# Recurrence stages: GpSimd makes two of the first query products, the state's blocks get banks of their own, and the modulation tiles move between the levels

## The reference

```python
def gla_chunk(q, k, v, logf, s0):
    ...
    b = jnp.cumsum(logf, axis=2)
    decay = jnp.where(mask, jnp.exp(jnp.where(mask, diff, 0.0)), 0.0)
    att = jnp.einsum('bnthk,bntshk,bnshk->bnhts', q, decay, k)
    o_intra = jnp.einsum('bnhts,bnshv->bnthv', att, v)
    ...
    def step(s, xs):
        o = jnp.einsum('bchk,bhkv->bchv', qc, s)
        s = dc[..., None] * s + jnp.einsum('bchk,bchv->bhkv', kc, vc)

def hgrn2_mix(q, iv, zf, zb, g, lbf, lbb, s0f, s0b):
    logf_f, k_f = forget_terms(zf, lbf)
    o_f, s_f = gla_chunk(q, k_f, iv, logf_f, s0f)
    logf_b, k_b = forget_terms(zb, lbb)
    o_b, s_b = gla_chunk(flip(q), flip(k_b), flip(iv), flip(logf_b), s0b)
    o = o_f + flip(o_b)
    ...

# per layer l:  (context rows first, then the latent rows, which start from the context's final states)
mod_x = (cond_x @ w_mod[l] + b_mod[l])[:, None, :]
yc, s_f, s_b = token_mixer(hc, ..., zero_state, zero_state, seq_conv)
yx, _, _ = token_mixer(hx, ..., s_f, s_b, latent_conv)
```

## Time and profile before

| | us |
|---|---|
| median of 3 runs | 4057.24 |
| the profiled execution's own time | 4046.82 |
| its span | 4045.0 |
| first recurrence | 226.5 to 275.2 |
| second recurrence | 275.2 to 338.3 |
| third recurrence | 2104.2 to 2161.4 |

### The profile page before, as it was taken

The page is one execution under the profiler, slowest core; times in us unless marked ns, Lnnn a source line. Parts: engine busy times, 40 slices in busy tenths (PEclk is TensorE's granted clock), DMA queues, the critical chain, the costliest instruction groups (busy, mean ns, idle before and its releaser), DMA issues. The chain is left out here.

```text
span 4045.0 us, 42202 instructions
## 1 busy us (share of the span) xinstructions
PE 3271.7 (81%) x13636; PEld 2079.7 (51%) x13636; DVE 2453.7 (61%) x5321; ACT 1372.9 (34%) x2942; POOL 1675.2 (41%) x1761
## 2 busy tenths in 40 slices
PE   6977986777777776677887777676779999999999
PEld 4845732223223332222576522232248978888788
DVE  4365746656556566665365755565557667676575
ACT  3364311112111111111365211111135566555664
POOL 0020566666666666666131566666630030000300
PEclk8989998888888888899998898898889999999999
DMA  5253699999999999999344899999964525455254
GB/s 194 104 220 124 228 365 354 371 364 363 368 359 361 372 361 365 353 365 378 135 157 167 325 376 353 377 358 364 372 247 176 207 84 188 177 181 202 84 188 146
DMA packets 247946, 1095.56 MB, mean 271 GB/s; under 512 B 28337, under 2 KB 31793, under 8 KB 228529
## 3 DMA queue, kind: packets, MB, share of 16 engines
q0 software_dynamic: 221184, 805.40, 51.8%
q1 hardware_dynamic: 26544, 287.47, 19.5%
HBM read 1091.72 MB, written 1.05 MB: 270 GB/s over the span
## 5 line engine op out<-in xcount | busy, mean ns | idle before, releaser
L2087 PE MATMUL ps<-v_rows,diagonal 128*128 128x512 f32 x3072 | 1542.4, 655 | 593.1 <-issue 271.0
L2087 PEld LDWEIGHTS ps<-v_rows,diagonal 128*128 128x128 f32 x3072 | 617.5, 209 | 1496.6 <-issue 1230.2
L1960 DVE CUSTOM_DVE_ANT_0 u_rows<-u_rows,ps 128x1024 f32<-128x1024 f32 x768 | 921.8, 1220 | 676.9 <-DMA u_rows<-in_u,experts 394.7
L1932 POOL DMA_INDIRECT v_rows<-in_v,experts x768 | 728.7, 949 | 482.0 <-issue 215.1
L1922 POOL DMA_INDIRECT u_rows<-in_u,experts x768 | 734.5, 956 | 341.9 <-issue 234.5
L2006 ACT ACTIVATE hidden<-hidden 128x2 f32<-128x2 f32 x384 | 77.5, 203 | 1716.0 <-DVEq L1962 865.7
L2842 PE MATMUL ps<-h_high_low,weights_high 128*128 128x512 f32 x1408 | 499.5, 400 | 6.5 <-DVE h_high_low L2697 6.3
L3265 DVE TENSOR_TENSOR weights_low<-ring,weights_high 128x1024 fp32r<-128x1024 f32 (+1 forms) x328 | 402.9, 1240 | 2.7 <-ACT weights_high L3258 2.5
L2843 PE MATMUL ps<-h_high_low,weights_low 128*128 128x256 f32 x1408 | 395.2, 281 | 0.0
L3258 ACT ACTIVATE weights_high<-ring 128x1024 fp32r<-128x1024 f32 (+1 forms) x328 | 338.7, 1033 | 99.7 <-PE ps L2843 54.1
L2842 PEld LDWEIGHTS ps<-h_high_low,weights_high 128*128 128x128 f32 x1408 | 265.4, 188 | 74.0 <-DVE h_high_low L2697 6.2
(11 more groups left out here) (357 smaller groups left out, 4029.1 us busy)
## 6 DMA issues: line engine op xcount, KB each, us to landing
ring<-in_ffn_gu SPq DMA_DIRECT2D x44, 2048.0 KB, 8.3
ring<-in_w_in SPq DMA_DIRECT2D x26, 2048.0 KB, 8.2
ring<-in_w_mod SPq DMA_DIRECT2D x24, 2048.0 KB, 9.5
ring<-in_ffn_down SPq DMA_DIRECT2D x32, 1408.0 KB, 6.0
ring<-in_peer_wq SPq DMA_DIRECT2D x8, 2048.0 KB, 8.6
u_rows<-in_u,experts POOLq DMA_INDIRECT x768
v_rows<-in_v,experts POOLq DMA_INDIRECT x768
ring<-in_w_out SPq DMA_DIRECT2D x4, 2048.0 KB, 10.2
```

The source lines that it names most:

```text
L1932: pool.indirect_dma_start(self.VROWS[n % self.v_slots][:, :], None, m.dram["v"], bass.IndirectOffsetOnAxis(ap=self.IDX[:, n:n + 1], axis=0 ...
L1960: dve.tensor_tensor_reduce(rows[:, :], rows[:, :], self.rows(), 1.0, 0.0, ALU.mult, ALU.add, self.HID[:, t % 2, s + r:s + r + 1])
L2087: mm = pe.matmul(self.A.ps[:, self.Y_BANK + half, :], self.DIAG[:, (g % DIAGONALS) * GROUP + r, :], rows[:, half * 512:(half + 1) * 512], ...
```

## The change

The line numbers of the changed kernel are up to 20 higher than those of the kernel before.

1. `first_vector` keeps two of its four query products on DVE (buffer 0). The two for buffer 1 become `first_copy`, which POOL makes ahead of its totals. ACT waits for them (`first_copied`) ahead of merge 1.
2. `FinalState` writes its turned rows to banks 1, 2, 3 and 7 and the state to banks 1 and 3. Its parts are placed apart: on PE the transposes open the stage, the state's products come behind level 1; on ACT `first_scalar` comes first, then the row copies, and the state is copied behind merge 2. PE waits for the copied state ahead of the final pass and no longer ahead of level 1.
3. `MOD_LEVELS` goes from (-1, -1, 1, 3, 4, 6, 7) to (-1, 0, 2, 4, 5, 7, 8).
4. ACT copies the modulation row behind the attention's last copy, and PE turns it behind the final pass (into bank 5, before bank 2).

```diff
-MOD_LEVELS = (-1, -1, 1, 3, 4, 6, 7)
+MOD_LEVELS = (-1, 0, 2, 4, 5, 7, 8)
...
+    TURN_BANKS = (1, 2, 3, 7)
+    STATE_BANKS = (1, 3)
...
-    def tensor(self, pe):
+    def tensor_rows(self, pe):
...
         mm.then_inc(m.e_turned.sem, 1)
+
+    def tensor_state(self, pe):
+        m, A = self.m, self.A
         pe.wait_ge(m.e_kept.sem, self.kept + 1)
...
     def gpsimd(self, pool, m):
 
+        self.first_copy(pool)
+        pool.drain().then_inc(m.first_copied.sem, 1)
         for level in range(1, LEVELS):
...
     def first_vector(self, dve):
         if self.queries:
-            for buf, right, d in ((0, 0, 1), (0, 1, 0), (1, 0, 0), (1, 1, 1)):
+            for buf, right, d in ((0, 0, 1), (0, 1, 0)):
                 dve.tensor_tensor(self.halves(self.QX[:, 1, buf, :, :], 1)[right], self.halves(self.q, 1)[right],
+                                  self.halves(self.total(1, d), 1)[right], ALU.mult)
+
+    def first_copy(self, eng):
+        if self.queries:
+            for right, d in ((0, 0), (1, 1)):
+                eng.tensor_tensor(self.halves(self.QX[:, 1, 1, :, :], 1)[right], self.halves(self.q, 1)[right],
                                   self.halves(self.total(1, d), 1)[right], ALU.mult)
...
         def _(act):
             if final is not None:
-                final.scalar_rows(act)
+                final.rows_turned(act)
             tree.first_scalar(act)
             act.drain().then_inc(m.act_a.sem, 1)
             if final is not None:
-                final.scalar_state(act)
+                final.scalar_rows(act)
             act.activation(G, G, ACT.Silu)
...
                 tree.pool_merged(act, m, level)
+                if level == 1:
+                    act.wait_ge(m.first_copied.sem, m.first_copied.at(1))
...
-                if level == LEVELS:
-                    beside.scalar(act)
+                if final is not None and level == 2:
+                    final.scalar_state(act)
...
             act.drain().then_inc(m.act_c.sem, 1)
+            beside.scalar(act)
...
             if final is not None:
-                final.tensor(pe)
+                final.tensor_rows(pe)
...
-                if final is not None and level == 1:
-                    final.ready(pe)
...
                 mm.then_inc(m.pe_a.sem, 1)
+                if final is not None and level == 1:
+                    final.tensor_state(pe)
                 beside.products_at(pe, level)
-            beside.turn(pe)
             pe.wait_ge(m.act_c.sem, m.act_c.at(1))
             if STATE is not None:
+                final.ready(pe)
...
             mm.then_inc(m.pe_b.sem, 1)
+            beside.turn(pe)
```

More of the change, by code:

```diff
@@ L1185, in tensor @@
                 n = 2 * dh + half
-                mm = pe.transpose(A.ps[:, 4 + n // 4, (n % 4) * P:(n % 4 + 1) * P], self.E[:, dh, half * P:(half + 1) * P],
+                mm = pe.transpose(A.ps[:, self.TURN_BANKS[n // 4], (n % 4) * P:(n % 4 + 1) * P], self.E[:, dh, half * P:(half + 1) * P],
                                   A.const[:, C_IDENT:C_IDENT + P])
         mm.then_inc(m.e_turned.sem, 1)
+    def tensor_state(self, pe):
+        m, A = self.m, self.A
         pe.wait_ge(m.e_kept.sem, self.kept + 1)
@@ L1192, in tensor, with rows_turned @@
             for half in range(2):
-                mm = pe.matmul(A.ps[:, 6 + dh // 4, (dh % 4) * P:(dh % 4 + 1) * P], self.KR[:, 2 * dh + half, :],
+                mm = pe.matmul(A.ps[:, self.STATE_BANKS[dh // 4], (dh % 4) * P:(dh % 4 + 1) * P], self.KR[:, 2 * dh + half, :],
                                self.IV[:, 2 * self.s + half, h * P:(h + 1) * P], start=(half == 0), stop=(half == 1))
         mm.then_inc(m.state_made.sem, 1)
+    def rows_turned(self, act):
+        act.wait_ge(self.m.e_turned.sem, self.turned + 1)
     def scalar_rows(self, act):
         m, A = self.m, self.A
-        act.wait_ge(m.e_turned.sem, self.turned + 1)
         for b in range(4):
-            act.activation(self.KR[:, 4 * b:4 * b + 4, :], A.ps[:, 4 + b, :].rearrange("p (n c) -> p n c", n=4), ACT.Copy)
+            act.activation(self.KR[:, 4 * b:4 * b + 4, :], A.ps[:, self.TURN_BANKS[b], :].rearrange("p (n c) -> p n c", n=4), ACT.Copy)
         act.drain().then_inc(m.e_kept.sem, 1)
@@ L1207, in scalar_state @@
         for b in range(2):
-            act.activation(self.STATE[:, 4 * b:4 * b + 4, :], A.ps[:, 6 + b, :].rearrange("p (n c) -> p n c", n=4), ACT.Copy)
+            act.activation(self.STATE[:, 4 * b:4 * b + 4, :], A.ps[:, self.STATE_BANKS[b], :].rearrange("p (n c) -> p n c", n=4), ACT.Copy)
         act.drain().then_inc(m.state_kept.sem, 1)
@@ L1529, in _ @@
             mm.then_inc(m.pe_b.sem, 1)
+            beside.turn(pe)
     m.totals.passed(LEVELS - 1)
+    m.first_copied.passed(1)
     m.merged.passed(LEVELS - Tree.POOL_FROM)
@@ L1617, in mixer @@
                     with ExitStack() as inner:
-                        beside = Modulation(m, A, BESIDE_MOD[layer][s], inner, bank=0, spot=2)
+                        beside = Modulation(m, A, BESIDE_MOD[layer][s], inner, bank=0, spot=5)
                         recurrence_stage(m, A, s, tree, IV, ATN, ATD, ATO, final, part(MIXR, 0, s), part(Q, 4, s), beside)
@@ L3506, in program @@
         m.conv_done, m.sigmoids = Signal(m, "conv_done"), Signal(m, "sigmoids")
+        m.first_copied = Signal(m, "first_copied")
         m.e_turned, m.e_kept, m.state_made, m.state_kept = (Signal(m, n) for n in ("e_turned", "e_kept", "state_made", "state_kept"))
```

## The result

The changed kernel takes 4033.44 us (median of five runs, 4029.99 to 4039.4) against 4057.24 for the one before (median of five, 4049.08 to 4064.48): a ratio of 0.9944, 95% interval 0.9932 to 0.9956. The forecast was 4042.7.

What follows compares the result with a forecast made beforehand. The prediction took waits between engines and, behind the opening, the ring of tile loads to bound the recurrences; 1.2 - 10.5 - 5.2 = -14.5 us against the median of 4057.2 gave 4042.7 us, range 4030 to 4056.

Steps and rivals of the forecast that it cites:

- The state's new place: Opening of second and third recurrence: merge 3 starts at 16.8 and 17.8 instead of 25.8 and 24.1, giving 9.0 and 6.3 us.
- The step from there to merge 3: Opening, from merge 1's end: merge 2 with its drains and DVE's emptying of a PSUM bank, put at 4.0 us.
- The second recurrence: Last tile decides, PE waiting for its load; final pass starts at 42.1, length 52.6 against 63.1, 10.5 us gained.
- j4 ends at 30.5, j6 at 43.5: First recurrence: modulation tile loads set the final pass's start; length 49.9 against 48.7, 1.2 us longer.
- The bare turn takes 1.1: 5.2 us gained: End of third recurrence: the uncovered modulation row turn takes 1.1 of the opening's 6.3 us, leaving 5.2 gained.
- GpSimd's products: Two query products moved off DVE, 1.0 us each on GpSimd: first recurrence loses about half a microsecond, the others nothing.
- merge 1 starts at 5.3: First recurrence's opening: with two products fewer, DVE starts merge 1 at 5.3 us instead of 6.6.
- The turns that the prediction worked through: Opening: DVE and POOL alternate on shared ports; a product is 0.55 us on DVE, 1.0 on POOL.
- rival (b): Opening: DVE and POOL don't really hinder each other; first recurrence's chain starts 2.4 us earlier, time 4040; chance 15%.
- (a): Recurrences: later tiles free load slots later, so the ring returns the gain; three slow hops, sum -3, time 4054; 13%.
- (c): Behind the recurrences: second `w_out` tile loads late, losing at most 4 us; time 4047; chance 8%.
- (d): GpSimd's strided products are slow: sign above 2.2 us each, 4.6 eats the gain, 6 gives 4065; chance 4%.

Runs made afterwards that it cites:

- e3: Kernel before with only the state's new order and banks (GpSimd's drain also stays ahead of its totals); three recurrences sum to 157.0 us.
- e12: Same kernel as e3, run again on another chip; three recurrences sum to 151.7 us.
- e8: Changed kernel run again unchanged; 4033.47 us (median of six), ratio 0.995 to the kernel before; three recurrences sum to 150.9 us.
- e11: Kernel before run again unchanged, on the third chip; three recurrences sum to 170.5 us.
- e10: Changed kernel with the old tile levels and all four query products on DVE, keeping the late row copy and turn; three recurrences sum to 152.5 us.
- e2: Changed kernel with only the old tile levels put back; three recurrences sum to 157.5 us.
- e7: e4 with the turn kept inside the final pass for seven tiles and ahead of it elsewhere; 4030.15 us, ratio 0.9943; recurrences sum to 147.0 us.
- e13: Same kernel as e7, run again on another chip; three recurrences sum to 147.7 us.
- e1: Changed kernel with GpSimd's two query products back on DVE; three recurrences sum to 148.3 us.
- e9: Same kernel as e1, run again on a second chip; three recurrences sum to 148.8 us.
- e4: e1 with GpSimd's totals waiting until DVE's sum and four products are done; three recurrences sum to 145.5 us.
- e5: Changed kernel with GpSimd's two query products made twice; three recurrences sum to 156.9 us.

## Why the prediction was right, and where its sizes were off

**The state's new place: right, and the main term.** It was to bring merge 3 to 16.8 and 17.8 in the second and third recurrence; it stands at 17.4 and 18.0, and with this edit alone at 16.9. By e3 and e12 it is worth a mean of 15.4 of the 19 us (169.8 to 154.4; by single pairs 12 to 19). Merge 1 ended at 12.3 and 13.5, about where it was forecast. The step from there to merge 3, put at 4.0 (which gives 16.4 in the second and not the 16.8 written), took 5.1 and 4.5.

**The second recurrence: right.** Forecast 52.6, measured 52.0 and 52.9. The final pass starts 42.1 behind the start, as worked out, and from there to the end it is 9.9 us where it was 8.8, so here the bare turn costs the 1.1 forecast. The path to that start was another, and that it ended at the same microsecond is luck. The forecast went by the even tiles, with a wait for the ring ahead of j6. The even tiles wait for nothing; j3, made behind level 4, ends at 25.1, j5's load starts then, PE waits 1.77 us for it and makes it at the slower clock until 37.5, and level 8 (which DVE's merges would have allowed at 35.8) and j6 follow. Whether j3 behind an earlier level would gain was not tried.

**The first recurrence: the sign was off.** The step "j4 ends at 30.5, j6 at 43.5" made the ring decide, at +1.2 us. The final pass starts at 42.4, the ring decides, but by j5 again:

```profile
261.18 3.60 PE L449 MATMUL ps<-ring,cond 128*32 128x512 f32 x16 [1.97 <-DMA ring<-in_w_mod]
265.16 2.02 PE L1518 MATMUL ps<-queries_scaled,keys_scaled 128*128 128x128 f32 x16 [0.38 <-issue]
```

j4 ended at 28.7 and j6 at 42.2. The length fell by 0.4 (48.34; 47.6 in e8, against 48.7 and 47.5 before), so within the scatter nothing changed.

**The third: the term for the bare turn was mis-sized.** The step "The bare turn takes 1.1: 5.2 us gained" took the final pass to be the same before and after. The final pass starts 6.2 us earlier, which is the opening's gain. But from there to the end before took 10.3 us and after takes 9.5, turn included. The windows around that place say why. Before:

```profile
2149.00:2151.00 2.00, 2.00 (x11) 1.99 (x10) 0.00 (x0) 1.98 (x4) 0.00 (x0) 0.50 0.79 336
2151.00:2153.00 2.00, 1.97 (x10) 1.88 (x10) 0.75 (x6) 0.05 (x1) 0.00 (x0) 0.50 0.10 41
2153.00:2155.00 2.00, 2.00 (x14) 2.00 (x14) 0.00 (x0) 0.00 (x0) 0.00 (x0) 0.68 0.03 8
```

And after:

```profile
2139.00:2141.00 2.00, 1.86 (x16) 1.86 (x16) 0.05 (x1) 1.22 (x3) 0.00 (x0) 1.00 0.98 356
2141.00:2143.00 2.00, 0.80 (x7) 0.64 (x6) 0.00 (x0) 1.68 (x3) 0.00 (x0) 1.00 0.92 360
2143.00:2145.00 2.00, 2.00 (x20) 2.00 (x19) 0.00 (x0) 0.00 (x0) 0.00 (x0) 1.00 0.96 360
```

The eighth column is the granted clock. Before, the final pass opened at 0.50, the 1.2 GHz level, and the turn ahead of it took 1.72 us; after it ran at 1.00, with PE at work on the last tile right ahead of level 8. Read in matmuls: 14 of them in a busy 2 us before, 20 after. In the first products of the pass:

```profile
2149.37 1.72 PE L464 MATMUL ps<-const,modulation_rows 128*128 128x12 f32 x8
2151.12 0.79 PE L1524 MATMUL ps<-att_diagonal,iv 128*128 128x128 f32 x2
```

```profile
2142.36 0.49 PE L1542 MATMUL ps<-att_diagonal,iv 128*128 128x128 f32 x2 [1.20 <-ACTq L1495]
```

The clock paid for the bare turn. The other runs give both sizes apart. All times are of the third recurrence, the clock is that of the pass' first four microseconds:

| kernels | levels | turn | pass starts | start to end | clock |
|---|---|---|---|---|---|
| before, e11 | old | early | 46.9, 49.6 | 10.3 | 0.50 to 0.71 |
| e3, e12 | old | early | 39.9, 40.0 | 10.4 | 0.50 to 0.65 |
| e10 | old | late | 39.4 | 11.1 | 0.50 to 0.72 |
| e2 | old | late | 40.0 | 9.5 | 1.00 |
| e7, e13 | new | early | 39.9, 39.5 | 8.8 | 1.00 |
| after, e8, e1, e9, e4, e5 | new | late | 39.5 to 43.4 | 9.5 | 1.00 |

At either clock the late turn costs 0.7 us here, not 1.1 (8.8 to 9.5, 10.4 to 11.1), and the slow clock costs 1.6 (8.8 to 10.4, 9.5 to 11.1). All eight executions with the new levels ran the pass at 1.00, and five of six with the old ones did not. That the tile's place keeps the clock up is an inference from this. e2 is the exception and stays open; the pause of PE ahead of the pass is not what sets it apart (1.79 us in e2, 1.70 in e3). It also explains the sign above: the third of e2 is 1.0 shorter than that of e10 by the clock, while its pass starts 0.6 later.

**GpSimd's products: right in sign, too small in size.** Forecast: half a microsecond lost in the first recurrence and nothing elsewhere, since ACT would hide it. Measured: some 2.2 in all by the means, of which only the 1.0 in the third stands clear of the scatter. Two steps failed. A product was put at 1.0 on GpSimd, with 2.02 as its bound; the two take 1.5 and 2.5, at line 1299 in the first recurrence:

```profile
L1299 POOL TENSOR_TENSOR queries_scaled<-q_g,z x1: 1525/1525/1525, 226.8 to 226.8; 128x512 f32<-128x512 f32 x1
L1299 POOL TENSOR_TENSOR queries_scaled<-q_g,z x1: 2500/2500/2500, 228.3 to 228.3; 128x512 f32<-128x512 f32 x1
```

And by "merge 1 starts at 5.3", against 6.6 before, DVE was to gain 1.3 from two products fewer. It gains 0.4, 6.2 against 6.6, since its sum became 2.6 long and its two products 3.4:

```profile
226.79 3.99 POOL L1299 TENSOR_TENSOR queries_scaled<-q_g,z 128x512 f32<-128x512 f32 x2 [192.31 <-POOLq L1035]
226.80 2.61 DVE L1446 TENSOR_TENSOR keys_scaled<-h 128x1024 f32<-128x1024 f32 x1 [4.98 <-PEq L1035]
229.33 3.44 DVE L1293 TENSOR_TENSOR queries_scaled<-q_g,z 128x512 f32<-128x512 f32 x2
232.97 2.83 DVE L1318 TENSOR_TENSOR keys_scaled<-keys_scaled,z 128x256 f32<-128x256 f32 x4 [0.19 <-issue]
233.85 5.10 POOL L1263 TENSOR_TENSOR decays<-decays 128x256 f32<-128x256 f32 x2 [0.18 <-issue]
```

The cover by ACT held in the third: ACT ends merge 1 at 13.5 in after, DVE at 12.8. What the third loses shows elsewhere. PE's level 4 starts 21.1 to 21.2 us behind the start with GpSimd's products and without, and takes 1.98 and 1.97 us in after and e8 against 1.15, 1.30 and 1.15 in e1, e9 and e4. First after, then e1:

```profile
2122.80 1.98 PE L1524 MATMUL ps<-queries_scaled,keys_scaled 128*64 128x64 f32 x32 [2.02 <-DVEq L1443]
```

```profile
2118.61 1.15 PE L1523 MATMUL ps<-queries_scaled,keys_scaled 128*64 128x64 f32 x32 [2.55 <-DVEq L1442]
```

So 0.8 of the 1.0 is one level at the slower clock, with the slow tile j3 right behind it. Whether the products bring that about no run separates. e5 shows the other price: with four products on GpSimd its queue holds up merge 1.

The turns that the prediction worked through are borne out by e4: take POOL away and the four products fall to 2.49. That DVE and GpSimd hold each other up is shown; rival (b) is refuted. (Merge 1 on DVE was to be over 6 us long; it took 4.9 in the first recurrence of after and 6.2 in that of e8.) The rule that it named (the Trainium skill, "SBUF — State Buffer", section "SBUF: two separate sides", one pair of ports held for a whole instruction) agrees with these rows: POOL's first product starts 0.01 us ahead and takes 1.53, and DVE's sum, 1.23 when it starts first, takes 2.61.

**The rivals.** (a) needed three slow hops of the ring and did not come: the second and third gained 11.0 and 7.0. (c) would have left up to 4 us behind the recurrences; e8 has 18.8 against 18.1 to 19.6 in the windows, but with an interval of 15 to 26, so a part of (c) stays possible. (d) needed 4.6 us for one product; the two take 1.5 and 2.5. The second is above the 2.2 that was named as its sign, and GpSimd's totals end at 16.4 in the first recurrence, right ahead of its half of merge 3 at 16.6: the slack was used up there. Why single tiles of the ring get the slower clock in one execution and not in another isn't settled by any run here.

## What to carry to other kernels

Where DVE and GpSimd hold each other up, as here, moving work from one to the other relieves little while both are at work: two products moved shortened DVE's opening by 0.2 us and lost 2.2 in all, by the means. Letting GpSimd start behind DVE's opening gave 1.8 us (mean of e4, e7 and e13 against e1 and e9). In a stretch bound by waits, follow the first long idle time back to what stands ahead of its releaser in that engine's list: the state's products, needed only later, moved behind level 1, and its row copies behind ACT's first copies, gave most of this gain. Compare the stretch's windows, take them twice before reading a term of one microsecond, and read the clock of the rows that differ before naming a cause.

## What the runs showed of the hardware that was not expected

- DVE's sum over 1024 elements takes 1.23 us when it starts first and 2.1 to 2.6 when POOL starts 0.01 us ahead of it: 226.49 against 226.48 in the earlier trace rows, 226.80 against 226.79 in after, but 226.33 against 226.41 in e1.
- POOL can be the one that is kept waiting: two totals of 256 elements took 5.10 us beside DVE's merge 1 (233.85 in the rows above), and 1.8 in the second and third recurrence of the same execution.
- The same 16 matmuls of a tile take 1.92 or some 3.6 us from one execution to the next of the same program (j0 of the first recurrence: 3.58 in after, 1.92 in e8); so do the 16 transposes that open the second recurrence:

```profile
272.88 3.38 PE L1188 MATMUL ps<-const,keys_scaled 128*128 128x128 f32 x16 [1.33 <-PEq L1424]
```

That is e1, against 1.94 in e9, the same kernel.

- One chip (e10 to e13) ran the whole program 6% faster, 3796.92 us for before, and the recurrences no faster. Its gathers moved more; before on the first chip, and then e11:

```profile
500.00:1500.00 1000.00, 739.86 (x1586) 312.27 (x1584) 594.21 (x1552) 179.57 (x572) 652.60 (x689) 0.89 0.95 362
```

```profile
500.00:1500.00 1000.00, 781.13 (x1791) 327.16 (x1790) 685.08 (x1776) 205.00 (x652) 738.94 (x783) 0.97 1.02 412
```

412 GB/s against 362 over the same thousand microseconds. Whole times of two kernels that ran on different chips can't be compared; the recurrences' windows can, within their scatter.
